# Score steps 0 to 3 of the prompt attention, two by two around halves of the last convolution job

## The reference, cut to what matters

```python
z = xn @ w_in                      # q, k, v, conv h, gate B, gate C
parts = [_dilated_prompt(q, k, v, w, d, slopes) for w, d in ((128,1), (512,4), (2048,16))]
attn_o = _merge_branches(parts)    # weights: the softmax denominators
u = gc * hc
conv_o = gb * (w_conv[0]*u[t-2] + w_conv[1]*u[t-1] + w_conv[2]*u[t])
h = x + concat(attn_o, conv_o) @ w_out
y = h + (silu(rms(h) @ w_gate) * (rms(h) @ w_up)) @ w_down
```

## Time and profile before

| what | value |
|---|---|
| median of three runs | 1224.04 us |
| the profiled execution's own time | 1223.98 us |
| its span in the trace | 1222.2 us |
| PE busy | 1206.4 us, 99% of the span |
| DVE, ACT, POOL busy | 604.0, 429.3, 512.6 us |
| granted clock of PE | 1.00 in the stretches around the change |

### The profile page before, as it was taken

The page is one execution under the profiler, slowest core; times in us unless marked ns, Lnnn a source line. Parts: engine busy times, 40 slices in busy tenths (PEclk is TensorE's granted clock), DMA queues, the critical chain, the costliest instruction groups (busy, mean ns, idle before and its releaser), DMA issues.

```text
span 1222.2 us, 22827 instructions
## 1 busy us (share of the span) xinstructions
PE 1206.4 (99%) x9323; PEld 1142.8 (94%) x9323; DVE 604.0 (49%) x1013; ACT 429.3 (35%) x810; POOL 512.6 (42%) x436
## 2 busy tenths in 40 slices
PE   7999999999999999999999999999999999999998
PEld 6998779889877799999999999999999999999998
DVE  6798324315577632479442424341111179756665
ACT  6111120010378811255333333333333444345452
POOL 3346023233144442042897777777777640000020
PEclk9999999999999999999999999999999999999999
DMA  5487656343233142010535455543222485222223
GB/s 212 143 298 239 233 199 272 138 169 128 78 110 104 54 178 70 1 36 36 189 141 191 174 190 174 190 139 122 71 88 71 155 337 220 92 91 95 81 77 107
DMA packets 67800, 174.00 MB, mean 142 GB/s; under 512 B 7088, under 2 KB 24176, under 8 KB 63472
## 3 DMA queue, kind: packets, MB, share of 16 engines
q1 hardware_dynamic: 67552, 172.27, 40.5%
q10 hardware_dynamic: 144, 0.27, 0.1%
HBM read 132.01 MB, written 40.51 MB: 141 GB/s over the span
## 4 chain that ended last, share of the span: by engine, by line
PE 52%; DVE 1%; issue 0%; ACT 0%; DVEq 0%; ACTq 0%
PE ps L1406 11%; PE ps L1408 11%; PE ps L1407 11%; PE ps L1432 6%; PE ps L1433 6%; PE ps L1434 6%; DVE combo_b L1995 0%; DVE w_lo L2391 0%; PE ps L1286 0%; DVE norms L1990 0%; PE ps L1278 0%; PE ps L1306 0%; DVE late L2504 0%; PE ps L1296 0%; DVE raw L2409 0%
## 5 line engine op out<-in xcount | busy, mean ns | idle before, releaser
L1406 PE MATMUL ps<-combo,w_hi 128*128 128x264 f32 x672 | 191.1, 284 | 0.0
L1408 PE MATMUL ps<-combo,w_lo 128*128 128x264 f32 x672 | 190.8, 284 | 0.0
L1407 PE MATMUL ps<-combo,w_hi 128*128 128x264 f32 x672 | 190.4, 283 | 0.0
L944 PE MATMUL ps<-act_hi,w_hi 128*128 128x352 f32 x480 | 157.5, 328 | 8.7 <-DVE act_lo L2000 8.7
L946 PE MATMUL ps<-act_hi,w_lo 128*128 128x352 f32 x480 | 154.6, 322 | 0.0
L945 PE MATMUL ps<-act_lo,w_hi 128*128 128x352 f32 x480 | 154.5, 322 | 0.0
L1432 PE MATMUL ps<-hid,w_hi 128*128 128x264 f32 x536 | 152.7, 285 | 0.0
L1433 PE MATMUL ps<-hid,w_hi 128*128 128x264 f32 x536 | 152.4, 284 | 0.0
L1434 PE MATMUL ps<-hid,w_lo 128*128 128x264 f32 x536 | 152.3, 284 | 0.0
L853 POOL TENSOR_TENSOR w_lo<-w_stage,w_hi 128x512 fp32r<-128x512 f32 (+1 forms) x71 | 99.3, 1399 | 122.5 <-ACT w_hi L1508 122.4
L1408 PEld LDWEIGHTS ps<-combo,w_lo 128*128 128x128 f32 x672 | 126.4, 188 | 0.0
(11 more groups left out here) (427 smaller groups left out, 2993.9 us busy)
## 6 DMA issues: line engine op xcount, KB each, us to landing
w_stage<-in_w SPq DMA_DIRECT2D x61, 512.0 KB, 3.6
resid<-in_state_k SPq DMA_DIRECT2D x8, 1792.0 KB, 10.6
v_buf<-in_state_v SPq DMA_DIRECT2D x14, 1024.0 KB, 6.5
h_d<-evac SPq DMA_DIRECT2D x44, 264.0 KB, 2.1
norms<-in_w SPq DMA_DIRECT2D x22, 512.0 KB, 4.4
t_d<-norms SPq DMA_DIRECT2D x11, 1024.0 KB, 7.5
resid<-in_xT SPq DMA_DIRECT2D x16, 528.0 KB, 7.1
raw<-in_w SPq DMA_DIRECT2D x14, 512.0 KB, 3.8
```

The source lines that it names most:

```text
L944: pe.matmul(out, hi, rhs_hi, start=first, stop=False)
L1406: pe.matmul(out, hi[:, wk], x_hi[:, k, tk], start=(k == 0 and first), stop=False, skip_group_check=not first)
L1407: pe.matmul(out, hi[:, wk], x_lo[:, k, tk], start=False, stop=False, skip_group_check=not first)
L1408: mm = pe.matmul(out, lo[:, wk], x_hi[:, k, tk], start=False, stop=(k == 3), skip_group_check=not first)
```

## The change

It moves instructions on PE, DVE and ACT; none is added or taken away, and POOL's and SP's lists stay as they are. The names are those of the list above.

```diff
             (PE)
-                if cj == 33:
-                    scores(0)
-
+
+            scores(0)
+            scores(1)
             conv_bank_free(CONV_JOBS - 1)
             last_conv_part(0)
-            scores(1)
             last_conv_part(1)
             pe.wait_ge(h_copied, 12)
             pe.wait_ge(c_used, 12)
+            pe.wait_ge(b_used, 11)
             scores(2)
+            scores(3)
             turn(0)
+            turn(1)
             last_conv_part(2)
-            pe.wait_ge(b_used, 11)
-            scores(3)
-            turn(1)
             last_conv_part(3)
             (ACT)
                     turned_copies(b)
+                    turned_copies(b + 1)
                     exponentials(b + 2)
-                    turned_copies(b + 1)
                     exponentials(b + 3)
                     conv_high(3)
             (DVE)
             conv_out(3, 0)
+            conv_out(3, 1)
             step_scores(0)
-            conv_out(3, 1)
             step_scores(1)
             reciprocals(0)
+            reciprocals(1)
             step_scores(2)
-            reciprocals(1)
             turned_copies(0)
             step_scores(3)
```

## The result

The changed kernel takes 1226.91 us (median of 14 runs, 1226.62 to 1228.64), the kernel before 1224.22 beside it (14 runs, 1223.88 to 1224.89): ratio 1.0023, 95% interval 1.0016 to 1.003, or +2.69 us. The forecast was +2.85 and 1226.8; that the second figure is met so closely is helped by the kernel before, which was 0.18 slower beside this run than in the three runs that the forecast started from. Two of the 21 executions of the kernel before beside the last two experiments took 1473 and 1689 us, at a mean granted clock of 0.75 and 0.66, and are left out.

A forecast was written before the change was run, and what follows sets the result against it. PE was taken to bound the kernel. Saved switches, three waits and ACT's lateness, -0.56 + 1.50 + 1.30 + 0.33 + 0.28 = +2.85 us, gave 1226.8 from 1223.98; own range 1226.4 to 1227.5, 8 in 10 range 1225.4 to 1227.7.

The forecast's parts named there:

- PE sets the end: Whole kernel: PE, busy 1206.4 of 1222.2 us, decides the time, so its list with waits is what counts.
- The switches save 0.56: PE around the end of the convolution: fewer changes between 64-row scores and 128-row convolution, -0.56 us.
- S1 waits, 1.50: Scores of step 1 on PE wait for DVE's two reads of step 0's scores: +1.50 us.
- S3 waits, 1.30: Scores of step 3 on PE wait for DVE's reads of step 2's scores: +1.30 us.
- Fill 3, 0.33: Last fill of the two transposed steps waits for the copy of fill 0: +0.33 us.
- ACT is late, 0.28: ACT's copy of the transposed sums comes 0.28 us later than the scores of step 4 do; counted in full.
- Nothing is given back: From step 5's scores on, lists stay equally late; PE's 0.52 us wait moves along. Rival, part given back: 0.16.
- The clock rival: PE's clock falls in the two new waits, nine matmuls run slow, 1.2 us more, 1228.0; chance 0.05.

The follow-up runs named there:

- the last two experiments: Bias table of next head pair's head 1 made earlier on DVE: with both score pairs together and their waits covered, 1222.92 us; alone on the kernel before, 1223.43.
- first_pair: Kernel before with only the scores of steps 0 and 1 put together and job 34's output read ahead on DVE: 1225.37 us against 1224.28 (1.0011).
- dve_order_back: Changed kernel with DVE taking job 34's output behind the scores of step 0 again: 1226.89 us against 1224.24 for the kernel before (1.0021).
- s3_other_half: Changed kernel with the scores of step 3 in the other two PSUM banks: 1225.55 us against 1224.28 for the kernel before (1.0011).
- long_wait: Changed kernel with DVE making head 1's bias table of the next head pair ahead of the scores of step 0: 1228.72 us against 1223.98 (1.0037).
- act_order_back: Changed kernel with ACT's list as before (fill 3's copy behind the exponentials of step 2): 1226.81 us against 1224.24 for the kernel before (1.0021).

## Why the prediction was right

- *PE sets the end.* Right: the shift of 2.75 at S5 is found again at the end of the span, 2.8.
- *The switches save 0.56.* Slightly too little: S2 and S3 together take 0.08 or 0.09 less than worked out, since the 0.89 of S3 counted a way in that it does not have behind S2. For S0 and S1 no run shows the pair without a wait. In the changed kernel the error has no effect, since S1 and S3 start when DVE is done, not when the set ahead has streamed; there they take 0.55 and 0.87, as if each stood alone.
- *S1 waits, 1.50.* With the 0.51 taken off, S1 starts at 323.86 (forecast 323.87). `first_pair` shows it alone, `dve_order_back` its 0.44 share (0.41 measured). Most of the rest is DVE's lateness too: had DVE been free, an estimate from the rows is S0 at 321.91, its read 0.67 later, 0.50 for the reads and 0.05 for the release, so S1 at 323.13 and a wait of 0.76 instead of 1.50.
- *S3 waits, 1.30.* It starts at 328.47 (328.48). `s3_other_half` removes it by removing the shared banks.
- *Fill 3, 0.33.* The wait is there, released as forecast, but its size is partly luck: the six transposes take 0.91 (forecast 0.60 + 0.33 = 0.93), of which the last four are 0.22 longer than before and the first two 0.08. So the wait is nearer 0.22, and the transposes cost some 0.09 more than six at 0.10; the two errors cancel. (The working also adds 329.37 + 0.38 + 0.27 to 330.05 instead of 330.02; the copy ended at 330.00.) S4 is 0.09 earlier than forecast: 0.03 stand already at the start of the transposes, as S3 takes 0.87 and not 0.89, 0.02 come in the transposes and 0.04 in parts 2 and 3.
- *ACT is late, 0.28.* The copy was 0.27 late against S4 in the trace after, S5 0.26, and both go when ACT's order is undone.
- *Nothing is given back.* Right: PE's wait at 340.47 moved along at the same length (0.51), as it belongs to DVE's backlog behind the scores of step 5. What the prediction did not name is what makes that backlog: the two bias tables, 2.46 us, of which `long_wait` had to move only one for the wait to go.
- *The clock rival* was not what happened in the profiled execution or the median. But falls do occur, in about one execution of ten by their times. The 1.2 us, read from nine matmuls at the start of the kernel, came near the 1.24 of the first part by luck, as nothing said that nine would be slow here too. The prediction treated the fall as an either-or; it is a lottery on top of the forecast. It is the likely reason of the upper end of the runs (1228.64, at a mean clock of 0.998).

## What to carry to other kernels

Before two jobs that share a PSUM bank are put side by side, hold the reader's whole turn against the time that the first one streams. Here the turn was 0.67 to 0.85 us from the start of the scores to the first read, then the reads and the release, and the stream 0.46 to 0.62. The saving was 0.56 as worked out, and the two exposed turns cost 1.50 and 1.30. Read the order on the reading engine as well: here it was late already, and of the 0.44 put ahead of the read 0.41 went into PE's wait. Paired over different banks, with dense work behind each pair, the same jobs kept the saving in the trace (0.35 and 0.53 at S4), though it is too small to be told in the time.

## What was not expected of the hardware

In one execution of act_order_back the granted clock fell to 0.50 while PE was busy, 1.1 us after it had taken up work again behind a wait of only 1.4 us in an otherwise dense stretch, and stayed low from 325.5 to 328.9 (worked out from the clock of 0.81 in the stretch that it ends in). The two profiled executions of the changed kernel have the same wait, 1.37, without the fall, and the kernel before, which never waits there, has no execution as late. What decides between them was not found. An estimate from these runs is that the wait costs its length and, now and then, 1.5 us more.
